# Delta rule on 32x32 blocks: the inverse's doubling products with four row and column groups

## The chip, the cores and the metric

The kernel runs on one core of a Trainium2 chip. The metric is the device time in microseconds (us) of one execution of the whole program, the median of three runs; a smaller number is better. A profile is one execution taken by the hardware profiler. Its engines are PE (TensorE's matmuls) and PEld (its weight loads, which overlap the matmuls), DVE (VectorE), ACT (ScalarE), POOL (GpSimd), and SP, which here issues DMAs only.

## The reference

One hybrid decoder layer: a combined projection, latent attention and a gated delta rule side by side, an output projection, and a gated convolutional feed-forward part. The change is in the delta rule alone. There the sequence is cut in chunks of 64 tokens, 33 of them, for four heads; for each chunk and head a unit lower triangular 64x64 matrix is inverted, and the state goes from chunk to chunk:

```
a_strict = jnp.einsum("bhnid,bhnjd->bhnij", k_beta, k) * decay * strict
t_inv = lax.linalg.triangular_solve(eye + a_strict, ..., lower=True, unit_diagonal=True)
u = t_inv @ v_beta;  w = t_inv @ (k_beta * exp(g))
...
v_new = u_c - w_c @ S
o = (q_c * exp(g_c)) @ S + qk_c @ v_new
S = S * exp(g_last) + (k_c * exp(g_last - g_c)).T @ v_new
```

`q` and `k` are divided by the root of their own square sums before this. All is float32.

## The kernel before

The program is a row of stages; stage_delta is the one that is changed. It lies between the short convolution and the attention, at about 693 to 1012 us of the profiled execution. It handles two chunks (`c` = 0, 1) at a time, which is called a tile here: 17 tiles, `t`. In a tile there are four units: two chunks times two pairs of heads. A unit holds two 64x64 matrices, one head on partitions 0 to 63 and one on 64 to 127 (`HALVES`).

The inverse is built by doubling. `xx` starts as the identity less the 2x2 blocks, as itself (half 0) and transposed (half 1). Each of five levels `lv` takes the off-diagonal blocks of its size from `nt[lv-1]` and forms, per head, P = `nt`·X (`first(lv)`, L1723), which ACT copies from the PSUM tile `pX` to `pr` (L1585), then X·P and its transpose (`second(lv)`, L1737 and L1739), which DVE adds to `xx` (L1641). Only then can the next level's `first` start. Levels 1 to 4 double blocks up to 32x32 and so touch nothing outside the 32x32 diagonal blocks of a matrix; level 5 fills the lower left 32x32 corner. The kernel before runs every product on the full 64x64 of a head, two heads side by side. ACT, DVE and PE do each level for chunk 0 and then for chunk 1.

Every engine runs a list of parts that `plain` writes out in a fixed order, tile after tile, with no loop left; a part stands with an offset, as (1, turn), the next tile's transpose. Engines meet in semaphores alone, so a part that waits holds all that stands behind it on its engine. PE's order in a tile is the last `plain` of the listing: between the products of the levels stand those of the state (`predict` L1770, `update` L1783, `outputs` L1796 and L1800, of the tile before), the next tile's `products` (L1699) and `turn` (L1709), the square sums of q of the tile after it (`q_norm`, L1688) and at the end `final` (L1750, L1755), which multiplies the inverse with v and k. DVE's order puts `state` (L1667, four instructions) ahead of the adds of level 2 and of level 5. ACT's order puts `turned` (L1579), the squares (L1543, L1544), the decays (L1567) and the copy of level 5 in one row, and then L1573 and `out(1)` (L1594), for whose end `final` waits.

Of the kernel before, what the change touches and what calls it, by code (L numbers as in the profile page):

```python
# [13 lines left out]
P = 128  # L14
# [784 lines left out]
def gates(nc, ctx, A, S, bank, ident, id_made):  # L799
# [32 lines left out]
    def load(pool):  # L832
# [3 lines left out]
        for hh in range(2):  # L836
            pool.dma_start(ab[hh * C2:hh * C2 + C2, 1:CHUNKS, :],
                          rows[N_META:L, :].rearrange("(c i) e -> i c e", i=CHUNK)).then_inc(loaded, 16)
            pool.dma_start(ab[hh * C2 + DN_PAD:hh * C2 + C2, 0, :], rows[0:N_META, :]).then_inc(loaded, 16)
        pool.dma_start(bias[:, :], A["dn_dt_bias"][0:1, :].to_broadcast([P, HEADS])).then_inc(loaded, 16)  # L840
# [10 lines left out]
    def masks_made(pool):  # L851
# [11 lines left out]
        for m in (tri, same, *only):  # L863
            step(pool.memset(m, 1.0))
        keep(only[0], [[0, P]], C2 - 1, -1)
        keep(only[1], [[0, P]], -C2, 1)
        keep(tri, [[1, P]], 0, -1)
# [466 lines left out]
GLB, NGC, ED, BETA = range(4)  # L1334
KINDS = 4
C2 = P // 2
HALVES = (slice(0, C2), slice(C2, P))
Q_LOG = -0.5 * float(np.log(P))


def stage_delta(nc, A, S):


    with ExitStack() as ctx:
        r = Room(nc, ctx, "dn")
        UH = UNITS * C2
        STEPS = LEVELS - 1
        LOADS = 3
        level_of, ident, off, eps, q_log, ones = (S[f"dn_{x}"] for x in ("level", "ident", "off", "eps", "q_log", "ones"))
# [6 lines left out]
        sqq = r.sb("sqq", [P, 2, HEADS, C2])  # L1356
# [12 lines left out]
        xx = [r.sb(f"xx{i}", [P, UNITS, 2, C2]) for i in range(2)]  # L1369
        nt = [r.sb(f"nt{i}", [P, STEPS, UNITS, C2]) for i in range(2)]  # L1370
        pr = r.sb("pr", [P, UNITS, C2])
# [5 lines left out]
        st = [r.sb(f"st{i}", [P, HEADS, P]) for i in range(2)]  # L1377
# [3 lines left out]
        pB = r.ps("pB", [P, 512])  # L1381
        pX = [r.ps(f"pX{i}", [P, 512]) for i in range(2)]
# [2 lines left out]
        pW = r.ps("pW", [P, 512])  # L1385
        pP = [p[:, 0:P].rearrange("p (u n) -> p u n", n=C2) for p in pX]
        pQ = [p[:, P:3 * P].rearrange("p (u x n) -> p u x n", u=2, x=2) for p in pX]
        pO, pV = pU[:, 0:2, :], pW[:, 0:2 * P].rearrange("p (g n) -> p g n", g=2)

        state_clear, loaded = r.sem("state_clear"), [S["dn_loaded0"]] + r.sems("loaded", LOADS - 1)  # L1390
        squared, qn_done, sums, logs, roots = (r.sems(x) for x in ("squared", "qn_done", "sums", "logs", "roots"))
# [217 lines left out]
        @block.vector  # L1609
        def _(dve):  # L1610
            dve.wait_ge(state_clear, 1)

            def square_sums(t, s, u):
                dve.wait_ge(squared[s], u + 1)
                dve.wait_ge(logs[s], u)
                dve.tensor_reduce(ss[s][:, 0:UNITS], sqk[:, :, :], AX.X, ALU.add)
                dve.wait_ge(qn_done[s], u + 1)
                dve.tensor_copy(ss[s][:, UNITS:], pB[:, UH:UH + UNITS]).then_inc(sums[s], 1)

            def strict(t, s, u):  # L1620
                dve.wait_ge(dec_strict[s], u + 1)
                dve.wait_ge(kk[s], u + 1)
                dve.wait_ge(x0_ready[1 - s], u + s)
                dve.wait_ge(bt_done[1 - s], u + s)
                dve.tensor_tensor(nn[:, 0, :, :], pK[:, :, 0, :], dec[:, 0, :, :], ALU.mult).then_inc(n_ready[s], 1)

            def attention(t, s, u):
                dve.wait_ge(dec_causal[s], u + 1)
                dve.wait_ge(o_done[1], t - 1) if t > 1 else None
                dve.tensor_tensor(qk[s][:, :, :], pK[:, :, 1, :], dec[:, 1, :, :], ALU.mult).then_inc(qk_ready[s], 1)  # L1630

            def level(lv):
                def run(t, s, u):
                    for c in range(2):
                        dve.wait_ge(q_done[c], STEPS * t + lv)
                        if lv == 1:
                            dve.wait_ge(x1_ready[s], u + 1)
                        x, q = xx[s][:, 2 * c:2 * c + 2, :, :], pQ[c]
                        if lv == STEPS:
                            x, q = x[:, :, 1, :], q[:, :, 1, :]  # L1640
                        dve.tensor_tensor(x, q, x, ALU.add).then_inc(x_step[c], 1)  # L1641
                return run

            def u_part(t, s, u):
                dve.wait_ge(u_done[s], 2 * u + 2)
                dve.tensor_copy(uu[s][:, :, :], pU[:, :, :]).then_inc(u_out[s], 1)

            def values(c):
                def run(t, s, u):
                    if c == 0:  # L1650
                        dve.wait_ge(u_out[s], u + 1)
                    dve.wait_ge(ws[c], t + 1)
                    dve.wait_ge(o_done[c], t)
                    dve.tensor_tensor(vn[c][:, :, :], uu[s][:, 2 * c:2 * c + 2, :], pV, ALU.subtract).then_inc(v_ready[c], 1)
                return run

            def state(c):
                def run(t, s, u):
                    dve.wait_ge(ks[c], t + 1)
                    if c == 0:  # L1660
                        dve.wait_ge(o_done[1], t)
                    else:
                        dve.wait_ge(o_done[0], t + 1)
                    dve.wait_ge(s_ready[1 - c], t + c)
                    for gg in range(2):
                        for hh in range(2):
                            o = dve.scalar_tensor_tensor(  # L1667
                                out=st[1 - c][:, 2 * gg + hh, :], in0=st[c][:, 2 * gg + hh, :],
                                scalar=egl[:, bass.ds(2 * t + c, 1), gg, hh], in1=pS[hh][:, gg, :],
                                op0=ALU.mult, op1=ALU.add)  # L1670
                    o.then_inc(s_ready[c], 1)
                return run

            plain(DT, (-1, values(0)), (0, level(1)), (-1, state(0)), (0, level(2)), (1, strict), (0, level(3)),
                  (-1, values(1)), (0, level(4)), (-1, state(1)), (0, level(5)), (2, square_sums), (1, attention), (0, u_part))

        @block.tensor
        def _(pe):
            pe.wait_ge(state_clear, 1)

            def q_norm(t, s, u):
                pe.wait_ge(squared[s], u + 1)
                pe.wait_ge(sums[1 - s], u + s)
                if t >= 1:
                    pe.wait_ge(bt_out[1 - s], u + s)
                for un in range(UNITS):
                    c, gg = un // 2, un % 2
                    m = pe.matmul(pB[:, UH + un:UH + un + 1], sqq[:, c, 2 * gg:2 * gg + 2, :].rearrange("p h i -> p (h i)"),  # L1688
                                  ones[:, :], start=True, stop=True)
                m.then_inc(qn_done[s], 1)  # L1690

            def products(t, s, u):
# [19 lines left out]
            def first(lv):  # L1712
                def run(t, s, u):
                    if lv == 1:
                        pe.wait_ge(x0_ready[s], u + 1)
                    pe.wait_ge(nt_ready[s], STEPS * u + lv)
                    for c in range(2):
                        pe.wait_ge(x_step[c], STEPS * t + lv - 1)
                        if STEPS * t + lv > 1:
                            pe.wait_ge(p_out[c], STEPS * t + lv - 1)  # L1720
                        for un in (2 * c, 2 * c + 1):
                            for rows in HALVES:
                                m = pe.matmul(pP[c][rows, un % 2, :], nt[s][rows, lv - 1, un, :], xx[s][rows, un, 0, :],  # L1723
                                              start=True, stop=True)
                        m.then_inc(p_done[c], 1)
                return run

            def second(lv):
                def run(t, s, u):
                    if lv == 1:  # L1730
                        pe.wait_ge(x1_ready[s], u + 1)
                    for c in range(2):
                        pe.wait_ge(p_out[c], STEPS * t + lv)
                        for un in (2 * c, 2 * c + 1):
                            if lv < STEPS:
                                for rows in HALVES:
                                    pe.matmul(pQ[c][rows, un % 2, 0, :], xx[s][rows, un, 1, :], pr[rows, un, :], start=True, stop=True)  # L1737
                            for rows in HALVES:
                                m = pe.matmul(pQ[c][rows, un % 2, 1, :], pr[rows, un, :], xx[s][rows, un, 1, :], start=True, stop=True)  # L1739
                        m.then_inc(q_done[c], 1)  # L1740
                return run

# [1928 lines left out]
```

## Time and profile before

| | before |
|---|---|
| median of 3 runs | 2991.72 us (2991.09 to 2991.76) |
| span of the profiled execution | 2990.1 us |
| PE busy over the span | 94% |
| mean granted TensorE clock | 0.974 of full speed |
| stage_delta, one tile in the steady part (835.92 to 853.48 us) | 17.56 us |

The profiled execution's span goes from its first to its last instruction; the median is 1.6 us above it. A row of the instruction list gives start, duration, engine, line, operation, what is written from what, shapes and count; merged rows of one kind cover several instructions. A form such as "64*64 64x64" is rows times columns of the weights, then the moving operand. A matmul's record goes from its start to the modelled end of its last result, so that records overlap, and a busy PE can still have room.

### The profile page before, as it was taken

Reading aid. Unit: us, or ns where it says so; the run is one execution under the profiler, and the core shown is the slowest. Engines: PE = TensorE matmul, PEld = TensorE weight load, DVE = VectorE, ACT = ScalarE, POOL = GpSimd, SP = SyncE. Lnnn points to the kernel's source line nnn. Section 1 sums busy time; section 2 is a strip of 40 time slices with the busy share of each in tenths; the row PEclk is TensorE's granted clock in tenths of the full one; section 3 lists DMA queues with packets and bytes.
Section 4 is the critical chain, followed back from the end, with each engine's and each line's share of the span. In section 5 each row is a group of like instructions: output and inputs, shape, how many; then the busy total and the mean of one; then the engine's idle time right before and its main releaser. Section 6 shows DMA issues by size and latency. Waiting matters only on the chain. (4 is left out here: it accounts for less than half of the span.)

```text
span 2990.1 us, 48834 instructions
## 1 busy us (share of the span) xinstructions
PE 2817.9 (94%) x18995; PEld 2440.4 (82%) x18995; DVE 1814.3 (61%) x2759; ACT 1181.2 (40%) x2210; POOL 1144.1 (38%) x1213
## 2 busy tenths in 40 slices
PE   7998979997999899998999599999999999999999
PEld 7997779996888688887788478888788888788887
DVE  3226834443555587777796677777887777543544
ACT  3226722223545365555443433333433333332321
POOL 2535930004776200001553456666666666100000
PEclk9999989997999899999999799999999999999999
DMA  8975953225454022221575633333533333654554
GB/s 269 354 251 171 263 166 111 67 74 130 108 147 87 22 75 91 85 68 40 179 246 164 216 93 105 95 103 94 190 105 99 101 105 97 240 170 146 192 167 142
DMA packets 403278, 421.07 MB, mean 141 GB/s; under 512 B 34075, under 2 KB 325995, under 8 KB 401000
## 3 DMA queue, kind: packets, MB, share of 16 engines
q1 hardware_dynamic: 368400, 298.61, 33.5%
q10 hardware_dynamic: 19944, 66.63, 6.8%
q0 software_dynamic: 14704, 52.69, 5.4%
q8 instruction: 153, 2.51, 0.3%
q14 instruction: 77, 0.63, 0.1%
HBM read 257.51 MB, written 160.34 MB: 140 GB/s over the span
## 5 line engine op out<-in xcount | busy, mean ns | idle before, releaser
L3526 PE MATMUL fu_pM<-fu_us_hi,fu_w_ring 128*128 128x512 f32 x2464 | 772.6, 393 | 15.2 <-DVE fu_us_lo L3361 14.3
L3526 PEld LDWEIGHTS fu_pM<-fu_us_hi,fu_w_ring 128*128 128x128 f32 x2464 | 466.3, 189 | 120.5 <-DVE fu_us_lo L3361 17.0
L3526 PE MATMUL fu_pM<-fu_us_lo,fu_w_ring 128*128 128x512 f32 x1232 | 482.8, 392 | 0.0
L3526 PEld LDWEIGHTS fu_pM<-fu_us_lo,fu_w_ring 128*128 128x128 f32 x1232 | 233.4, 189 | 47.8
L3262 ACT ACTIVATE fu_w_ring<-fu_sw 128x512 fp32r<-128x512 f32 x176 | 110.9, 631 | 325.3 <-PE fu_pM L3526 264.1
L3368 DVE TENSOR_TENSOR fu_w_ring<-fu_sw,fu_w_ring 128x512 fp32r<-128x512 f32 x132 | 139.4, 1056 | 65.4 <-ACT fu_w_ring L3262 65.3
L3368 DVE TENSOR_TENSOR fu_w_ring<-fu_w_raw,fu_w_ring 128x512 fp32r<-128x512 f32 x88 | 108.5, 1233 | 104.3 <-ACT fu_w_ring L3262 104.3
L2995 PE MATMUL fu_pM<-fu_us_hi,fu_w_ring 128*128 128x512 f32 x666 | 169.3, 391 | 1.3 <-DVE fu_w_ring L2918 1.3
L3262 ACT ACTIVATE fu_w_ring<-fu_w_raw 128x512 fp32r<-128x512 f32 x132 | 83.0, 629 | 191.3 <-PE fu_pM L3526 169.9
L3409 DVE SCALAR_TENSOR_TENSOR fu_acc<-fu_gb,fu_taps,fu_acc 128x1024 f32<-128x1024 f32 x88 | 133.0, 1513 | 37.7 <-ACT fu_acc L3303 36.9
L2075 ACT ACTIVATE at_pt_hi<-at_pT 128x512 fp32r<-128x512 f32 (+3 forms) x176 | 92.7, 539 | 143.6 <-PE at_pT L2340 142.7
L2918 DVE TENSOR_TENSOR fu_w_ring<-fu_w_ring 128x1408 fp32r<-128x1408 f32 x37 | 60.6, 1639 | 146.1 <-ACT fu_w_ring L2867 146.1
L2995 PEld LDWEIGHTS fu_pM<-fu_us_hi,fu_w_ring 128*128 128x128 f32 x666 | 125.8, 189 | 28.0 <-DVE fu_w_ring L2918 1.8
L2995 PE MATMUL fu_pM<-fu_us_lo,fu_w_ring 128*128 128x512 f32 x555 | 144.4, 392 | 4.0 <-DVE fu_w_ring L2918 4.0
L3219 POOL TENSOR_TENSOR fu_w_ring<-fu_w_raw,fu_w_ring 128x512 fp32r<-128x512 f32 x44 | 60.3, 1370 | 227.1 <-ACT fu_w_ring L3262 227.1
L2209 DVE TENSOR_TENSOR at_pt_lo<-at_pT,at_pt_hi 128x512 fp32r<-128x512 f32 (+3 forms) x176 | 106.2, 615 | 52.8 <-ACT at_pt_hi L2075 51.6
L2995 PEld LDWEIGHTS fu_pM<-fu_us_lo,fu_w_ring 128*128 128x128 f32 x555 | 105.1, 190 | 26.3 <-DVE fu_w_ring L2918 4.4
L2867 ACT ACTIVATE fu_w_ring<-fu_w_ring 128x1408 fp32r<-128x1408 f32 x37 | 51.0, 1379 | 182.7 <-PE fu_pM L2995 157.5
L1641 DVE TENSOR_TENSOR dn_xx<-dn_pX,dn_xx 128x256 f32<-128x256 f32 (+1 forms) x170 | 65.1, 397 | 78.1 <-PE dn_pX L1739 75.8
L2340 PE MATMUL at_pT<-id_ident,at_row 128*128 128x128 f32 x608 | 94.1, 276 | 13.5 <-ACT at_row L2067 11.8
L1469 POOL MEMSET dn_st<- 128x512 f32 x1 | 0.5, 524 | 276.3 <-POOLq L1017 276.3
L3219 POOL TENSOR_TENSOR fu_w_ring<-fu_sw,fu_w_ring 128x512 fp32r<-128x512 f32 x44 | 77.0, 1750 | 66.2 <-ACT fu_w_ring L3262 66.2
(539 smaller groups left out, 7141.5 us busy)
## 6 DMA issues: line engine op xcount, KB each, us to landing
fu_w_ring<-scr_gs ACTq DMA_DIRECT2D x37, 704.0 KB, 4.6
fu_w_raw<-in_w_gate SPq DMA_DIRECT2D x22, 1024.0 KB, 5.4
fu_w_raw<-in_w_up SPq DMA_DIRECT2D x22, 1024.0 KB, 5.4
scr_gs<-fu_sg SPq DMA_DIRECT2D x84, 256.0 KB, 3.0
scr_gs<-fu_acc SPq DMA_DIRECT2D x63, 256.0 KB, 2.9
fu_us_lo<-scr_gs ACTq DMA_DIRECT2D x19, 704.0 KB, 4.6
pj_wd<-in_w_down POOLq DMA_DIRECT2D x11, 1024.0 KB, 9.3
scr_td<-pj_td POOLq DMA_DIRECT2D x11, 1024.0 KB, 8.0
```

What stands on the lines that cost most here:

```text
L1641: dve.tensor_tensor(x, q, x, ALU.add).then_inc(x_step[c], 1)
L2075: act.activation(pt_hi[x % NPX][:, at:GW], pT[TURN[n, m] % NPT][:, :, :].rearrange("p i n -> p (i n)")[:, at:GW], ACT.Copy).then_inc(hi_do ...
L2209: dve.tensor_tensor(pt_lo[x % NPX][:, at:GW], pT[TURN[n, m] % NPT][:, :, :].rearrange("p i n -> p (i n)")[:, at:GW], f(pt_hi[x % NPX][:, a ...
L2340: t = pe.transpose(pT[x % NPT][:, i, :], rows[n % 2][i][:, at:at + P], ident[:, :])
L2867: act.activation(a_hi[s], f(a_lo[s]), ACT.Copy).then_inc(a_half, 1)
L2918: dve.tensor_tensor(a_lo[s], f(a_lo[s]), f(a_hi[s]), ALU.subtract).then_inc(a_ready, 1)
L2995: m = pe.matmul(pM[(U + e) % BANKS][:, :], a[s][:, j, :], x[c][j], start=(j == 0 and n_pass == 0), stop=(j == PAIRS - 1 and n_pass == 2))
L3219: pool.tensor_tensor(w_lo[q % RING][:, :, :], operand(ph % 2, i), f(w_hi[q % RING][:, :, :]), ALU.subtract).then_inc(w_ready_pool, 1)
L3262: act.activation(w_hi[q % RING][:, :, :], operand(m, i), ACT.Copy).then_inc(w_half, 1)
L3368: dve.tensor_tensor(w_lo[q % RING][:, :, :], operand(ph % 2, i), f(w_hi[q % RING][:, :, :]), ALU.subtract).then_inc(w_ready, 1)
L3409: dve.scalar_tensor_tensor(out=out, in0=gb[:, row, j:j + 2 * B], scalar=tap, in1=out, op0=ALU.mult, op1=ALU.add).then_inc(convolved[row] i ...
L3526: p = pe.matmul(bank(2 * n + m, i)[:, :], a[:, k, :], x[:, k, :], start=(k == 0 and n_pass == 0), stop=(k == HALVES_K - 1 and n_pass == 2))
```

## The change

Levels 1 to 4 run each product on the four 32x32 diagonal blocks of the 128 partitions (`BLOCKS`: block b has rows and columns of the array from 32b on), where two 64x64 blocks stood. Level 5 runs its two products on the 32x32 corner of each head alone (`CORNERS`), and writes the second to a PSUM region of its own, `pE`. Since DVE and ACT still read whole 64x64 regions, two products of zeros clear both banks of `pX` at the stage's start. `q_norm` is written as two products of 64 weight columns per unit, one for each half of the output partitions, where one of 128 columns stood.

```diff
@@ stage_delta
+        pE = [p[:, 3 * P:4 * P].rearrange("p (u n) -> p u n", n=C2) for p in pX]
+        BLOCKS = [(slice(b * QT, b * QT + QT), slice(b % 2 * QT, b % 2 * QT + QT)) for b in range(P // QT)]
+        CORNERS = [(BLOCKS[2 * hh], BLOCKS[2 * hh + 1]) for hh in range(2)]
...
@@ def level (DVE)
-                            x, q = x[:, :, 1, :], q[:, :, 1, :]
+                            x, q = x[:, :, 1, :], pE[c]
...
@@ def _(pe)
             pe.wait_ge(state_clear, 1)
+            for bank in pX:
+                pe.matmul(bank[:, :], st[0][:, 0, :], st[0][:, :, :].rearrange("p h d -> p (h d)"), start=True, stop=True)
...
@@ def q_norm
-                    m = pe.matmul(pB[:, UH + un:UH + un + 1], sqq[:, c, 2 * gg:2 * gg + 2, :].rearrange("p h i -> p (h i)"),
-                                  ones[:, :], start=True, stop=True)
+                    for hh, rows in enumerate(HALVES):
+                        m = pe.matmul(pB[rows, UH + un:UH + un + 1], sqq[:, c, 2 * gg + hh, :], ones[:, :], start=True, stop=True)
...
@@ def first
-                            for rows in HALVES:
-                                m = pe.matmul(pP[c][rows, un % 2, :], nt[s][rows, lv - 1, un, :], xx[s][rows, un, 0, :],
-                                              start=True, stop=True)
+                            if lv < STEPS:
+                                for rows, cols in BLOCKS:
+                                    m = pe.matmul(pP[c][rows, un % 2, cols], nt[s][rows, lv - 1, un, cols], xx[s][rows, un, 0, cols],
+                                                  start=True, stop=True)
+                            else:
+                                for (top, left), (low, right) in CORNERS:
+                                    m = pe.matmul(pP[c][low, un % 2, left], nt[s][top, lv - 1, un, right], xx[s][top, un, 0, left],
+                                                  start=True, stop=True)
...
@@ def second
-                                for rows in HALVES:
-                                    pe.matmul(pQ[c][rows, un % 2, 0, :], xx[s][rows, un, 1, :], pr[rows, un, :], start=True, stop=True)
-                            for rows in HALVES:
-                                m = pe.matmul(pQ[c][rows, un % 2, 1, :], pr[rows, un, :], xx[s][rows, un, 1, :], start=True, stop=True)
+                                for rows, cols in BLOCKS:
+                                    pe.matmul(pQ[c][rows, un % 2, 0, cols], xx[s][rows, un, 1, cols], pr[rows, un, cols],
+                                              start=True, stop=True)
+                                for rows, cols in BLOCKS:
+                                    m = pe.matmul(pQ[c][rows, un % 2, 1, cols], pr[rows, un, cols], xx[s][rows, un, 1, cols],
+                                                  start=True, stop=True)
+                            else:
+                                for (top, left), (low, right) in CORNERS:
+                                    m = pe.matmul(pE[c][top, un % 2, right], pr[low, un, left], xx[s][low, un, 1, right],
+                                                  start=True, stop=True)
```

On PE, level 4 with `turn` between its two halves: `first` writes `dn_pX` from `dn_nt`, `turn` writes `dn_pB`, and of `second` the first unit is shown. Before:

```order
L1723 MATMUL dn_pX<-dn_xx,dn_nt 64x64 x8
L1709 MATMUL dn_pB<-cd_ident,dn_nn 64x64 x8
L1737 MATMUL dn_pX<-dn_pr,dn_xx 64x64 x2
L1739 MATMUL dn_pX<-dn_xx,dn_pr 64x64 x2
L1737 MATMUL dn_pX<-dn_pr,dn_xx 64x64 x2
```

The same place now:

```order
L1730 MATMUL dn_pX<-dn_xx,dn_nt 32x32 x16
L1715 MATMUL dn_pB<-cd_ident,dn_nn 64x64 x8
L1748 MATMUL dn_pX<-dn_pr,dn_xx 32x32 x4
L1751 MATMUL dn_pX<-dn_xx,dn_pr 32x32 x4
L1748 MATMUL dn_pX<-dn_pr,dn_xx 32x32 x4
```

Nothing changes its place; each product of two halves is now four blocks, and `turn`, which stays at 64x64, stands between groups of another size.

On PE, level 5 and the end of a tile: `outputs` writes `dn_pU` (twice), `second(5)` writes `dn_pX`, then `q_norm` writes `dn_pB` and `final` starts with `dn_pU`. Before:

```order
L1723 MATMUL dn_pX<-dn_xx,dn_nt 64x64 x8
L1796 MATMUL dn_pU<-dn_st,dn_qt 64x128 x4
L1800 MATMUL dn_pU<-dn_vn,dn_qk 64x128 x4
L1739 MATMUL dn_pX<-dn_xx,dn_pr 64x64 x8
L1688 MATMUL dn_pB<-cd_ones,dn_sqq 128x1 x4
L1750 MATMUL dn_pU<-dn_vb,dn_xx 64x128 x8
```

The same place now:

```order
L1734 MATMUL dn_pX<-dn_xx,dn_nt 32x32 x8
L1813 MATMUL dn_pU<-dn_st,dn_qt 64x128 x4
L1817 MATMUL dn_pU<-dn_vn,dn_qk 64x128 x4
L1755 MATMUL dn_pX<-dn_xx,dn_pr 32x32 x8
L1695 MATMUL dn_pB<-cd_ones,dn_sqq 64x1 x8
L1767 MATMUL dn_pU<-dn_vb,dn_xx 64x128 x8
```

Level 5 keeps its eight products and has them smaller; `q_norm` has eight in place of four.

## Rows read from the trace of the kernel before

**Rows 1.** Busy us of PE, PEld, DVE, ACT, POOL; granted clock; DMA; two stretches.

```profile
770.00:810.00 40.00, 39.46 (x834) 34.47 (x836) 20.77 (x59) 18.51 (x66) 29.62 (x44) 1.00 0.53 124
835.90:853.46 17.56, 17.29 (x362) 15.06 (x360) 9.04 (x25) 8.69 (x31) 12.49 (x19) 1.00 0.57 144
```

**Rows 2.** Waits within that one tile: us in total, times, longest.

```profile
ACT dn_pr L1585 <- PE dn_pX L1723: 4.6, 4, 2.8
DVE dn_xx L1641 <- PE dn_pX L1739: 4.0, 4, 1.8
```

**Rows 3.** PE in order of time, one tile: start, duration, instruction, count.

```profile
835.92 0.68 PE L1723 MATMUL dn_pX<-dn_xx,dn_nt 64*64 64x64 f32 x16
838.68 0.87 PE L1723 MATMUL dn_pX<-dn_xx,dn_nt 64*64 64x64 f32 x16
842.23 0.68 PE L1723 MATMUL dn_pX<-dn_xx,dn_nt 64*64 64x64 f32 x16
842.84 0.66 PE L1796 MATMUL dn_pU<-dn_st,dn_qt 128*64 128x128 f32 x8
843.43 0.65 PE L1800 MATMUL dn_pU<-dn_vn,dn_qk 64*64 64x128 f32 x8
844.03 0.28 PE L1739 MATMUL dn_pX<-dn_xx,dn_pr 64*64 64x64 f32 x4
...
844.73 0.28 PE L1739 MATMUL dn_pX<-dn_xx,dn_pr 64*64 64x64 f32 x4
845.53 0.68 PE L1723 MATMUL dn_pX<-dn_xx,dn_nt 64*64 64x64 f32 x16
848.19 0.68 PE L1723 MATMUL dn_pX<-dn_xx,dn_nt 64*64 64x64 f32 x16
850.43 1.05 PE L1688 MATMUL dn_pB<-cd_ones,dn_sqq 128*128 128x1 f32 x8
851.42 1.09 PE L1750 MATMUL dn_pU<-dn_vb,dn_xx 64*64 64x128 f32 x16
853.48 0.33 PE L1723 MATMUL dn_pX<-dn_xx,dn_nt 64*64 64x64 f32 x4
```

**Rows 4.** All products of L1723 in the stage: count, busy us, mean ns.

```profile
L1723 PE MATMUL dn_pX<-dn_xx,dn_nt 64*64 64x64 f32 x1360 | 63.1, 229 | 3.3 <-issue 1.2 <-DVE dn_xx L1641 0.3
```

**Rows 5.** PE and its loads in order of time, at four places.

```profile
850.43 0.97 PEld L1688 LDWEIGHTS dn_pB<-cd_ones,dn_sqq 128*128 128x128 f32 x8
852.44 0.97 PEld L1755 LDWEIGHTS dn_pS<-dn_xx,dn_kbg 64*128 64x128 f32 x16 [0.17 <-issue]
1035.99 1.06 PE L2388 MATMUL at_pO<-da_vm_raw,at_sm_turned 16*16 16x128 f32 x8 [0.30 <-ACT at_sm_turned L2130]
1684.39 1.07 PE L3538 MATMUL fu_pM<-fu_w_raw,fu_head 128*32 128x256 f32 x16
```

**Rows 6.** ACT and DVE in order of time, the same tile.

```profile
836.04 0.66 ACT L1602 ACTIVATE dn_wt<-dn_pS 128x256 f32<-128x256 f32 x2 [2.88 <-PE dn_pS L1755]
840.24 1.12 DVE L1667 SCALAR_TENSOR_TENSOR dn_st<-dn_st,cd_egl,dn_pS 128x128 f32<-128x128 f32 x4 [1.20 <-PE dn_pS L1783]
841.28 0.75 DVE L1641 TENSOR_TENSOR dn_xx<-dn_pX,dn_xx 128x256 f32<-128x256 f32 x2
846.73 0.39 ACT L1579 ACTIVATE dn_nn<-dn_pB 128x256 f32<-128x256 f32 x1 [0.19 <-PE dn_pB L1709]
850.09 0.63 ACT L1594 ACTIVATE dn_osb<-dn_pU,dn_qscale 128x128 f32<-128x128 f32 x2
```

**Rows 7.** The stage's start in order of time.

```profile
695.37 1.84 PE L1688 MATMUL dn_pB<-cd_ones,dn_sqq 128*128 128x1 f32 x8 [10.29 <-ACT dn_sqq L1544]
705.04 1.42 POOL L1479 TENSOR_TENSOR dn_offs<-dn_grow,cd_off 128x256 f32<-128x256 f32 x2 [4.29 <-DMA dn_gall<-scr_gcr]
```

**Rows 8.** Two stretches of tile 0, columns as in rows 1.

```profile
712.60:716.00 3.40, 1.75 (x44) 1.54 (x46) 0.55 (x3) 1.48 (x7) 3.40 (x8) 1.00 0.00 0
716.00:719.40 3.40, 3.40 (x48) 2.93 (x46) 0.75 (x2) 0.56 (x2) 3.40 (x5) 0.50 0.70 192
```

More of the change, by code:

```diff
@@ L1336 @@
 C2 = P // 2
+QT = P // 4
 HALVES = (slice(0, C2), slice(C2, P))
```

## The prediction

> **What bounds the kernel now.** The change touches stage_delta alone, so I read that stage. First the table of stretches: in the steady part PE is busy 39.46 of 40.00 us and 17.29 of 17.56 us in one tile, at the full clock [rows 1]; the other engines are busy about half the time or, POOL, 71%. Then the waits of that tile: the longest on ACT and DVE are for PE's products of the inverse, 4.6 and 4.0 us [rows 2]. PE orders the stage, and the tile takes 17.56 us, from one first product to the next [rows 3].
>
> A busy PE need not be full, since records overlap, so I need what a product costs. Each float32 product shows two passes: 680 products of L1723 give 1360 records [rows 4]. In a dense run, from 844.03 to 844.73, six groups of four passes start 0.70 us apart, 29.2 ns for each pass [rows 3]. Are two halves side by side in that? Eight loads of 128 weight columns on all rows take 0.97 us, and sixteen on alternating halves take 0.97 us too [rows 5]; eight passes of 128 columns on one small tile take 1.06 us [rows 5], sixteen on two halves 1.09 [rows 3]. So two halves run together, and the unit is a slot: one pass on both halves, 58.3 ns for 64 columns. Sixteen passes of 256 columns on four column groups take 1.07 us [rows 5], twice the columns of L1750 in the same time: four run together there.
>
> **The change, part by part.** *Products.* A tile's inverse has 112 products before: 224 passes, 112 slots, 6.53 us of PE. After, levels 1 to 4 have 192 products in 96 slots of four, and level 5 has 16 in 16 slots of two: 112 slots again, with half the weight and half the moving columns. No row shows a 32x32 slot. Its lower bound is half, 29.2 ns. Its upper bound is that passes never come faster than now: four times 29.2, 116.7 ns, and 58.3 at level 5. It is nearest to the four column groups, which keep pace with their columns; I take 36 ns, the half and some 7 ns for two more starts per slot (an estimate). Saved: 112 x 22.3 ns = 2.50 us of PE a tile.
>
> The Trainium skill speaks against this: "TensorEngine Tiling (Array Packing)", Instruction Overhead, gives each matmul some 60 cycles whatever its free size and says not to take a tiling factor from a dimension that is already small. By it 416 passes of 25 ns would be 10.4 us where 6.53 stood, about +4 us a tile (an estimate from that page). The rows above show passes on different parts of the array started together, so whether that floor is the engine's or one block's no row here settles. It is the first rival below.
>
> *q_norm.* Eight passes with 128 weight columns take about 0.97 us; sixteen with 64 are eight slots, 0.47 us by the slot above. Saved 0.45 us with the ends.
>
> *Sizes that change.* Where PE goes from one tile size to another it loses time: L1796 begins at 842.84 and L1800 at 843.43 [rows 3], 0.59 us for four slots of 109 ns (L1750's 128 columns), so 0.15 us. After the change `turn` stands alone at 64x64 between 32x32 groups, and L1800 no longer has the size of the products behind it: four more such steps, +0.60 us a tile.
>
> *Zeros.* Two products of 512 columns at the start, four passes. L3538's 256 columns give about 0.22 us a pass, so 0.9 us at half speed for 512, 3.5 us in all. They hold the first `q_norm` of 695.37 by 1.5 us or so; but tile 0 waits on POOL, which itself waited for a load until 705.04 [rows 7]. I cost them at nothing. Without that cover they cost 1.5 us. `pE` is as large as what DVE read; nothing.
>
> *Sum on PE:* 2.50 + 0.45 - 0.60 = 2.35 us a tile. Over 17 tiles 40 us: the ceiling, 2952 us.
>
> *What the path gives.* Once PE is quicker, the chain product, copy, product, add is bare in places, so I walk the tile, first product to first product of the levels [rows 3].
> - Level 1, 2.76 us. The second product starts after ACT's `wt` copies (836.04 on) and two more ACT steps [rows 6], not after the first. Only chunk 0's half of the second shortens what follows: -0.18.
> - Level 2, 3.55. `update` starts some 0.09 earlier still, then `state` on DVE, 1.12 us, and only behind it the adds at 841.28 [rows 6]. PE's second is 0.36 shorter, and the next tile's `products` fill most of the wait: the next first can start at about 841.6. -0.45.
> - Level 3, 3.30. Second -0.36, first -0.13, one more step of size +0.15: -0.34.
> - Level 4, 2.66. First -0.08, second -0.36, two steps of size, 0.06 for the copy: -0.19.
> - Level 5, 2.24. -0.18, +0.10, -0.13: -0.21.
> - `q_norm` to the next tile, 3.05. PE would give -0.38. But `final` (851.42) waits for ACT's `out(1)` (850.09 to 850.72), and ACT works in one row from `turned` (846.73) to it [rows 6], 3.99 us. That row starts when `turn` does, about 1.0 us earlier, so `final` starts at about 849.77: -0.28.
>
> Together -1.65, a tile of 15.9 us. The other 0.7 us of PE's gain turns into waits for ACT and DVE. A slot of 29.2 ns would give about -1.8, one of 44 ns -1.25; at 57 ns the products save 0.15 and, with `q_norm`, no more than the steps of size cost.
>
> Sixteen tile lengths stand between the 17 first products: 16 x 1.65 = 26.4 us. I take 3 off for a lower clock now and then (second rival): 23.4. The span becomes 2990.1 - 23.4 = 2966.7; the median lay 1.6 above the span, so 2968 us.
>
> **Rivals.**
> 1. *Passes stay at 29.2 ns each* (issue, not the array, sets the pace). Then 416 passes cost 12.1 us where 6.53 stood, +5.6 - 0.45 + 0.60 = +5.75 a tile, +92 us over 16: 3084. It decides once a slot of four takes over 57 ns. For it: no row has passes closer on average in a long run. Against it: four column groups at once [rows 5]. A slot between 50 and 60 ns would give within 10 us of before.
> 2. *The clock falls in the thin part.* In tile 0, PE busy for 1.75 of 3.40 us was followed by a half clock, at which 48 passes took 3.40 us [rows 8]. After the change PE is thinnest from the first product to `update`, some 3.3 us: I count 1.6 us of columns in it, 2.3 of 3.6 before. If the clock halves there in each tile, that work takes twice as long, up to 1.6 us: the whole gain, 2991. In half of the tiles, 2979. If it stays low through the stage, most of the 14.9 us of PE's work left in a tile (17.29 - 2.35) doubles: over 3100.
> 3. *The chain hides more than I walked.* If ACT and DVE start no earlier than now but for level 2 and the last part, about -0.7 a tile: 2980.
>
> **How the numbers follow.** A measurement here can tell about 0.2% (6 us) from no change. My forecast, four together and ACT's row the next bound, 2957 to 2975: 0.55. The third rival, 2975 to 2984: 0.12. The second, 2979 to 2992: 0.14, two in five of it within 0.2%. A slot near break-even, within some 10 us of before: 0.05. The first rival, or a clock that stays low: 0.14, slower. Faster is 0.55 + 0.12 + 0.08 + 0.01 = 0.76, same 0.06 + 0.03 = 0.09, slower 0.15. The range from 2955 (the ceiling less three) to 2996 leaves out the first rival and a little at the low end.
>
> **What would show it.** Right: 32x32 products in groups of four passes every 36 ns or so, some 15.9 us a tile, waits of PE for `dn_xx` and `dn_pr`, `final` waiting for `dn_osb`, and the clock at 1.00 through the steady part. Wrong: groups of four no closer than 58 ns (first rival); stretches of the stage at 0.50 (second); a tile above 16.5 us at the full clock with short products (third). The rest of the program should only start earlier.

## The result and the profile after

The changed kernel takes 3062.18 us (median of four runs, 3051.91 to 3064.01); the kernel before, timed beside it, 2991.74 (2991.09 to 2992.59). The ratio is 1.0231, 95% interval 1.0214 to 1.0248: slower by 2.3%, 94 us above the forecast and 66 us above its range. The profiled execution, the shortest of the four, took 3051.91 us, its span 3050.2. The span grew by 60.1 us, and all of it lies in stage_delta: from the start of the first tile's `products` to that of the last it takes 345.1 us, 284.9 before.

The view to open first is that of stretches, for the changed kernel: busy us of PE, PEld, DVE, ACT and POOL, then the granted clock, the DMA share and GB/s. The first row is the stretch of [rows 1], the second one tile, the others lie inside that tile.

```profile
770.00:810.00 40.00, 35.46 (x967) 29.42 (x964) 14.27 (x39) 13.14 (x50) 20.17 (x31) 0.65 0.39 86
905.86:926.98 21.12, 17.70 (x563) 14.35 (x561) 8.90 (x25) 8.60 (x31) 12.52 (x19) 0.84 0.47 122
910.70:914.10 3.40, 1.59 (x63) 1.38 (x63) 1.13 (x4) 0.00 (x0) 2.64 (x4) 1.00 0.74 206
914.10:917.50 3.40, 3.19 (x93) 2.34 (x83) 0.71 (x2) 1.07 (x4) 1.45 (x2) 0.50 0.83 170
917.50:920.90 3.40, 3.40 (x107) 2.82 (x107) 0.85 (x2) 0.83 (x4) 0.00 (x0) 0.50 0.35 96
```

Where the clock stood at 1.00 it is now 0.65 in the first row, and PE is idle for 4.54 us of 40 where it was idle for 0.54. A tile takes 21.12 us in place of 17.56, and holds 563 PE records and 561 of PEld in place of 362 and 360 (a float32 product shows as four records: two passes, each with a weight load on PEld). The third row is the one to keep in mind: at the full clock PE was busy for only 1.59 of 3.40 us, and after it come two stretches at half clock.

Why was PE idle there? The waits of that tile (us in total, times, longest):

```profile
ACT dn_pr L1589 <- PE dn_pX L1730: 7.0, 2, 4.7
DVE dn_xx L1645 <- PE dn_pX L1751: 6.8, 5, 2.6
...
PE dn_pX L1748 <- issue: 2.5, 2, 2.2
```

ACT and DVE wait for PE's products longer than before [rows 2], although each is shorter, and PE's longest wait is put down to "issue", that is, to nothing that the profile shows. PE in order of time around it (start, duration, instruction, count, idle before):

```profile
909.05 0.71 PE L1800 MATMUL dn_pS<-dn_vn,dn_kd 64*128 64x128 f32 x8
909.70 0.26 PE L1748 MATMUL dn_pX<-dn_pr,dn_xx 32*32 32x32 f32 x8
...
910.11 0.21 PE L1751 MATMUL dn_pX<-dn_xx,dn_pr 32*32 32x32 f32 x2
912.51 0.23 PE L1748 MATMUL dn_pX<-dn_pr,dn_xx 32*32 32x32 f32 x4 [2.20 <-issue]
```

The stop of 2.20 us falls in the middle of one chunk's second products, where the program has no wait at all: the products before and after it are of one unit, and their operands were ready before the chunk began. What moved then is seen in the view of the DMA queues (packets, MB, share of 16 engines). Three rows of it: the stretch from 910.0 to 911.2, then 730 to 970 in this kernel, then 730 to 970 in the kernel before:

```profile
q8 instruction: 1, 0.02, 5.5%
q8 instruction: 49, 0.80, 1.4%
q8 instruction: 39, 0.64, 1.1%
```

Queue q8 carries instructions. Its one packet from 910.0 to 911.2, 16,384 bytes, started at 910.06 and took 1.05 us; PE ran another 13 records, stopped at 910.31 and went on at 912.51. That is the pattern everywhere: between 860 and 1000 PE stops 12 times for over 0.6 us, and each stop ends 2.3 to 3.0 us after the start of such a packet. Between 730 and 970 the queue carried 49 packets where the kernel before had 39, for 12,272 and 9,814 records of PE and PEld: 250 and 252 records a packet.

So the reading to test: PE's program is delivered in packets of some 250 records, a packet can be used 2.3 to 3.0 us after its transfer starts, and a row of blocks is used up sooner. Theory A says that this is the loss and that the half clock comes behind these stops. Theory B is the prediction's second rival: the blocks leave PE too few columns, and the clock falls for that.

### The profile page after: what moved, and what is told of

Same layout as the page of the kernel before. It is cut to its first block and busy times, and to the rows that moved or that the text cites. A ratio compares the mean times of both kernels' runs of the same rounds, so it can differ in the third digit from the quotient of the medians.

```text
span 3050.2 us, 55642 instructions
## 1 busy us (share of the span) xinstructions
PE 2835.7 (93%) x22399; PEld 2437.7 (80%) x22399; DVE 1808.6 (59%) x2759; ACT 1180.1 (39%) x2210; POOL 1144.8 (38%) x1213
```

## The experiments

All are timed against the kernel before on the same chip; the pattern of the first two is a square: the changed kernel has thin products (few columns) and many instructions, the kernel before thick ones and few, and each of these two has one of each.

**Thin products, few instructions.** The changed kernel, with one product of 64 rows and 32 columns for each half in place of two blocks (the same in `second`, and at level 5 in place of the corners, whose result DVE then reads from `pQ` again):

```diff
-for rows, cols in BLOCKS:
-    m = pe.matmul(pP[c][rows, un % 2, cols], nt[s][rows, lv - 1, un, cols], xx[s][rows, un, 0, cols], start=True, stop=True)
+for hh, rows in enumerate(HALVES):
+    top, left = BLOCKS[2 * hh]
+    m = pe.matmul(pP[c][top, un % 2, left], nt[s][rows, lv - 1, un, left], xx[s][rows, un, 0, left], start=True, stop=True)
```

> The changed kernel, but each 64x64 product of the inverse is cut to its upper left 32x32 (64 rows, 32 weight columns, 32 moving columns, one product for each half as before): about half of PE's columns in the products, as in the changed kernel, but 112 products a tile and not 208. It leaves out three quarters of each product's output, so the inverse is not computed. Theory A (instructions arrive too slowly: PE runs dry in the middle of groups, and these stops take the clock down): no stop over 0.6 us within a group in the steady part, granted clock 1.00 in nearly all of the stage, a tile of 15.5 to 16.5 us, 2955 to 2980 us. Theory B (the clock falls because the products keep too few columns busy, with or without stops): no stops either, but the clock at half in a third of the stage or more, a tile over 17.5 us, over 2995 us.

It takes 2973.26 us, ratio 0.9935 (0.992 to 0.995). The stretches, of the steady part and of one tile, of this kernel:

```profile
730.00:970.00 240.00, 219.60 (x5496) 180.55 (x5494) 127.70 (x373) 125.23 (x454) 185.50 (x280) 0.98 0.50 116
828.32:843.69 15.37, 14.43 (x375) 11.89 (x369) 8.53 (x26) 8.47 (x31) 12.49 (x20) 1.00 0.73 166
```

With the changed kernel's thin work the clock is 0.98, and a tile without a long stop takes 15.37 us. Theory B's fall does not come. Theory A was not quite right either: it expected no long stop, and there are seven over 0.6 us between 730 and 970. Shorter products alone use up instructions faster (738 records in 15.37 us, where 722 took 17.56), and the tiles are 15.4 to 17.8 us long.

**Thick products, many instructions.** The kernel before, each product cut into two by its weight columns, so that four run side by side on 64 rows and 32 columns:

```diff
-for rows in HALVES:
-    m = pe.matmul(pP[c][rows, un % 2, :], nt[s][rows, lv - 1, un, :], xx[s][rows, un, 0, :], start=True, stop=True)
+for (rows, cols), half in zip(BLOCKS, (HALVES[0], HALVES[0], HALVES[1], HALVES[1])):
+    m = pe.matmul(pP[c][rows, un % 2, :], nt[s][half, lv - 1, un, cols], xx[s][half, un, 0, :], start=True, stop=True)
```

> The kernel before, each 64x64 product of the inverse cut into two by its weight columns (64 rows, 32 weight columns, all 64 moving columns; four run side by side): the computation and PE's columns are those of before, but there are 224 products a tile in place of 112, so PE has some 1190 records a tile in place of 740. Theory A (instructions arrive too slowly): stops of 1 to 3 us in the middle of groups, one or two a tile, more than 20 us over the stage, and stretches at half clock behind them: 3020 to 3080 us. Theory B (too few columns): the clock stays at 1.00, no more than the steps of tile size are lost (0.3 to 0.6 us a tile): 2992 to 3003 us.

It takes 3054.98 us, ratio 1.021 (1.0196 to 1.0224): theory A's case. PE in order of time, a run of its second products, and then the stretch of the steady part:

```profile
830.18 0.29 PE L1739 MATMUL dn_pX<-dn_pr,dn_xx 64*32 64x64 f32 x8
830.29 0.29 PE L1742 MATMUL dn_pX<-dn_xx,dn_pr 64*32 64x64 f32 x8
...
830.52 0.27 PE L1742 MATMUL dn_pX<-dn_xx,dn_pr 64*32 64x64 f32 x3
831.54 0.31 PE L1742 MATMUL dn_pX<-dn_xx,dn_pr 64*32 64x64 f32 x5 [0.75 <-issue]
```

```profile
730.00:970.00 240.00, 209.19 (x6480) 170.89 (x6480) 100.97 (x276) 98.21 (x346) 137.94 (x209) 0.96 0.43 100
```

Eight passes take 0.11 us, 57 ns for four side by side with 64 columns: the array does its work at the pace of before. The same computation with the same columns is 2.1% slower because each product comes in two pieces, and PE stops in the middle of a group of eight. From the first `products` to the last it takes 52.5 us more than the kernel before, and PE's idle time put down to "issue" between 690 and 1080 is 35 us more: most of this loss is stops. The rest is left for the clock (0.96) and the steps of tile size, which this kernel has too.

**The sums of squares alone.** The kernel before with the change to `q_norm`:

```diff
-m = pe.matmul(pB[:, UH + un:UH + un + 1], sqq[:, c, 2 * gg:2 * gg + 2, :].rearrange("p h i -> p (h i)"), ones[:, :], start=True, stop=True)
+for hh, rows in enumerate(HALVES):
+    m = pe.matmul(pB[rows, UH + un:UH + un + 1], sqq[:, c, 2 * gg + hh, :], ones[:, :], start=True, stop=True)
```

> The kernel before with the sums of squares alone on two column groups (8 products of 64 weight columns in place of 4 of 128), all products on 64x64. Both theories: no change of the clock and no stops. By the walk of the prediction, PE is 0.45 us quicker behind level 5, and the final products then wait for the copy of the outputs on ACT: between nothing and 0.4 us a tile, 2984 to 2992 us.

It takes 2983.98 us, ratio 0.9973 (0.9964 to 0.9982), at the better end of the expectation: a tile of 17.13 us against 17.55, by the starts of `products`, and no stop over 0.6 us in the steady part.

**Corners and sums of squares.** The changed kernel with levels 1 to 4 on 64x64 again (in `first`, and the same in `second`):

```diff
 if lv < STEPS:
-    for rows, cols in BLOCKS:
-        m = pe.matmul(pP[c][rows, un % 2, cols], nt[s][rows, lv - 1, un, cols], xx[s][rows, un, 0, cols], start=True, stop=True)
+    for rows in HALVES:
+        m = pe.matmul(pP[c][rows, un % 2, :], nt[s][rows, lv - 1, un, :], xx[s][rows, un, 0, :], start=True, stop=True)
```

> The changed kernel with levels 1 to 4 on 64x64 again: only level 5 runs on 32x32 corners (16 products, as many as before) and the sums of squares run on two column groups (8 products in place of 4). Theory A: 16 more records a tile bring no stops; level 5 saves 16 slots of some 22 to 26 ns, 0.35 to 0.4 us, the sums of squares up to 0.45, and the new steps of size take about half of that back; 0.2 to 0.5 us a tile, 2980 to 2988 us, the clock at 1.00. Theory B: the thinner end of the tile already takes the clock down in some tiles: 2990 us or more.

It takes 2981.85 us, ratio 0.9968 (0.9956 to 0.9981), the fastest here but for the thin kernel, which leaves work out. The interval overlaps that of the sums of squares alone; the profile tells the corners' share, 16.80 us against 17.13 in the commonest tile, 17.01 against 17.34 on average. Its stretch, and the end of one tile in PE's order of time:

```profile
730.00:970.00 240.00, 235.45 (x5222) 202.01 (x5222) 126.44 (x356) 120.66 (x435) 177.34 (x269) 1.00 0.49 115
```

```profile
857.41 0.44 PE L1734 MATMUL dn_pX<-dn_xx,dn_nt 32*32 32x32 f32 x16
858.95 0.44 PE L1755 MATMUL dn_pX<-dn_xx,dn_pr 32*32 32x32 f32 x16
859.32 0.63 PE L1695 MATMUL dn_pB<-cd_ones,dn_sqq 128*64 128x1 f32 x16
```

Both products of level 5 take 0.44 us in place of the first's 0.68 [rows 3], the sums of squares 0.63 in place of 1.05. So those two parts of the change are worth having; what is left to blame is the blocks of levels 1 to 4.

**How many instructions are too many.** Four kernels stand between the corners kernel and the changed one. They put the blocks of 32x32 back for a part of levels 1 to 4, here for the second products of level 3:

```diff
-if lv < STEPS:
+if lv in (3,):
+    for rows, cols in BLOCKS:
+        pe.matmul(pQ[c][rows, un % 2, 0, cols], xx[s][rows, un, 1, cols], pr[rows, un, cols], start=True, stop=True)
+    for rows, cols in BLOCKS:
+        m = pe.matmul(pQ[c][rows, un % 2, 1, cols], pr[rows, un, cols], xx[s][rows, un, 1, cols], start=True, stop=True)
+elif lv < STEPS:
     for rows in HALVES:
...
```

> The corners kernel (level 5 on corners, sums of squares on two column groups) and, at levels 1 to 4, 32x32 blocks for the first products alone: 32 products more, some 884 records a tile against 756 (and 1124 in the changed kernel). Theory A (a packet of 256 instructions comes some 2.4 us after it is asked for, and PE stops where it has used up the half it still has): in the first products the block groups are followed by a wait for ACT, so few stops, 0 to 10 us in all; the eight slots a level save 0.2 us each, part of it on the path: 2970 to 2990 us. Theory B (too few columns): less than a tenth of PE's columns are gone, the clock stays, no stops: 2968 to 2978 us.

> The corners kernel and, at levels 1 to 4, 32x32 blocks for the second products alone: 64 products more, some 1012 records a tile, 64 of them in a row in each chunk. Theory A: stops of 1 to 3 us in most tiles, 20 to 40 us in all, and stretches at half clock: 3000 to 3045 us. Theory B: twice the columns of the first products are gone; if that alone takes the clock, stretches at half clock without stops ahead of them; if not, 2960 to 2975 us.

> The corners kernel and 32x32 blocks for the second products of levels 2 and 4 alone: 32 products more, as many records a tile (884) as with all first products on blocks, but in two runs of 128. Theory A: if the count in a short time matters, more stops than with the first products, 5 to 20 us in all; what the blocks save on the path (0.3 to 0.7 us a tile) is about given back: 2972 to 2995 us. Theory B: the clock stays and nothing stops: 2968 to 2978 us.

> The corners kernel and 32x32 blocks for the second products of level 3 alone: 16 products more, 820 records a tile, one run of 128 a tile between the outputs and the predict group, which run at 25 ns a record or slower. Theory A: a stop only where a packet is asked for just ahead of the run, in some tiles, under 8 us in all; the blocks save up to 0.36 us a tile: 2973 to 2985 us. Theory B: no stops, 2975 to 2980 us.

In the kernel with blocks in the first products alone, the second products read beside the diagonal blocks what level 5 of the tile before left in `pP`, which changes the computation but no instruction. The expectations' counts are 18 to 20 a tile higher, as they take in waits (but not the 1124 of the changed kernel); the table has records of PE and PEld alone, 722 before [rows 1] and 4 for each product added. Clock and stops are those of the stretch 730 to 970, stops being PE's idle time put down to "issue". Short idle times, most of them ahead of a first product, are in that column too: stops of over 0.6 us come to 6.9 us in the thin kernel, 7.5 to 7.7 in the three behind it, then 29.6, 27.3 (changed) and 26.3, and to nothing in the first three rows. Each ratio is to the kernel before on the chip of that run, where its median was 2992.83 (the first four experiments) or 2992.49 us (the last four).

| kernel | records a tile | time, us | ratio (95%) | clock | stops, us |
|---|---|---|---|---|---|
| before | 722 | 2991.74 | 1 | 0.99 | 0.2 |
| sums of squares alone | 738 | 2983.98 | 0.9973 (0.9964 to 0.9982) | 1.00 | 0.2 |
| corners, sums of squares | 738 | 2981.85 | 0.9968 (0.9956 to 0.9981) | 1.00 | 0.8 |
| thin, few | 738 | 2973.26 | 0.9935 (0.992 to 0.995) | 0.98 | 13.8 |
| second, level 3 | 802 | 2989.10 | 0.9997 (0.9989 to 1.0006) | 0.99 | 8.6 |
| first, levels 1 to 4 | 866 | 2986.46 | 0.9981 (0.9972 to 0.9989) | 0.96 | 9.2 |
| second, levels 2 and 4 | 866 | 2986.82 | 0.9982 (0.9974 to 0.9991) | 0.96 | 10.8 |
| second, levels 1 to 4 | 994 | 3038.66 | 1.0149 (1.0134 to 1.0165) | 0.83 | 33.4 |
| changed | 1122 | 3062.18 | 1.0231 (1.0214 to 1.0248) | 0.77 | 31.9 |
| thick, many | 1170 | 3054.98 | 1.021 (1.0196 to 1.0224) | 0.96 | 27.2 |

Theory A's case again, with two misses. The second products of level 3 alone were expected between 2973 and 2985 us with under 8 us of stops, and took 2989 with 8.6: already 64 records a tile bring seven stops of over 0.6 us between 730 and 970 and give back what the corners had won. And the two kernels with 866 records do not differ, so the count in a tile told more here than how I had spread it. Theory B has no account of the first of these: only the second products of one level are thinner there, the clock is 0.99, and the gain is gone all the same.

Two things in these traces settle more than the times do. First, where PE stops. The seven kernels with stops have 84 of over 0.6 us between 730 and 970. From one such stop to the next in the same kernel there is always a whole number of packets, with 248 to 252 records of PE and PEld for each (in the changed kernel, for example, 252, 252, 754, 1004, 1258), and just as many packets start their transfer in between. So PE stops at the end of a packet, when the next one is not there yet, and each stop ends 2.2 to 3.2 us after that packet's start. After a stop, the next transfer starts only 1.0 to 3.4 us later: while PE uses one packet, only the one after it is on its way. Where two stops lay one packet apart, they were 3.7 us apart at the least.

Second, when the clock falls. In the ten kernels it fell from full to half speed 27 times between 730 and 970, ten of them in the changed kernel. Each time PE was in a stop of over 0.6 us or had ended one at most 2.5 us before; in the three kernels without such stops it never fell there. Theory B's fall without stops is in none of these stretches.

## Why the prediction was wrong, point by point

- **The slot: right.** 36 ns taken (29.2, and 7 for two more starts, which no row showed), bounds 29.2 and 116.7; 32 measured. Four groups of eight passes of the changed kernel at the full clock, start and duration:

```profile
896.16 0.24 PE L1751 MATMUL dn_pX<-dn_xx,dn_pr 32*32 32x32 f32 x8
896.23 0.24 PE L1748 MATMUL dn_pX<-dn_pr,dn_xx 32*32 32x32 f32 x8
896.29 0.24 PE L1751 MATMUL dn_pX<-dn_xx,dn_pr 32*32 32x32 f32 x8
896.35 0.25 PE L1748 MATMUL dn_pX<-dn_pr,dn_xx 32*32 32x32 f32 x6
```

  From 896.16 to 896.35 six slots go by in 0.19 us: 32 ns for four passes, 8 ns for one. The first rival falls: passes on different blocks do not hold each other to 29.2 ns. The Trainium skill's "TensorEngine Tiling (Array Packing)", Instruction Overhead, gives each matmul some 60 cycles; as a price for each of several products side by side it does not agree with these rows.
- **The sums of squares: right on PE, too low on the path.** 0.45 us forecast for PE, 1.05 against 0.63 found; the walk let 0.28 of it through, and the tile gained 0.42.
- **The walk: right in kind, a little too careful.** It gave 15.9 us a tile. The thin kernel, with as many slots and the same steps of tile size, runs a tile without long stops in 15.37. Sixteen tiles shorter by 2.18 us each would be 35 us, 2957 in all. By that kernel, which starts two products side by side where the changed one starts four, this much of the gain is there on the array; in the changed kernel itself no run shows it free of stops.
- **The zeros: right.** They took 3.78 us (3.5 forecast), and PE's first level product starts at 708.64, at 708.73 before.
- **The step that failed: "112 slots again, with half the weight and half the moving columns".** The sum costed the products as slots of the array and nothing else. It saw 208 products where 112 stood and never asked how their instructions reach PE. "Issue" came in only as a pace of the passes (the first rival), and that pace was fine. What took its place was not a price for each pass but stops at the ends of instruction packets: 15 of over 0.6 us for the 49 packets between 730 and 970, 27.3 us, and with the short ones 31.9 us in some 11 tiles, 2.9 us a tile, more than the 1.65 us that the walk had won. The half clock behind them, and what waits for PE then, took about as much again, by subtraction (next point).
- **The clock: taken as 3 us, and the second rival had its cause wrong.** That rival let the clock fall wherever PE is thin. The thin kernel has that thinness and the clock at 0.98; it is 0.77 in the changed kernel, where thinness and many long stops meet. In the tile shown above the stop comes first, the half clock after it, and so with all ten falls between 730 and 970. Stops with thick products take it only to 0.96, but those stops are shorter too: none over 1.9 us, where seven of the changed kernel's 15 last over 2.0. The price of the clock by itself was not measured: a tile of the changed kernel is 21.57 us long on average (by the starts of `products`), 6.2 above 15.37, of which idle time put down to "issue" is 2.9, and the remaining 3.3 is left for the half clock and what waits for PE then, by subtraction.
- **The third rival** can't be judged from the changed kernel. In the thin kernel PE is busy for 14.43 of 15.37 us; the chain hid less than that rival feared.

The Trainium skill does bear on the failed step, though the prediction did not draw on it there: "Runtime: NRT & Kernel Launch", Instruction fetch mechanics, says that instructions come in blocks of 16 KiB, 256 of them, fetched ahead, and that the cost of crossing a block is mostly hidden because the sequencer dispatches more slowly than blocks arrive. The size agrees (16,384 bytes, some 250 records and the waits among them). That the crossing is hidden holds in the kernel before, 0.2 us of stops in 240, at 24 ns a record (17.56 us by 722). It does not hold here, where a dense row of blocks has eight records every 32 ns.

What stays open: why a packet's transfer starts now 1.0 and now 3.4 us after PE has begun the packet ahead of it, and why none starts sooner. In the twelve stops between 860 and 1000 PE ran from 0 to 142 records between the packet's start and the stop, and in two of them the packet started only after PE had stopped. Open too is what takes the clock as far down as 0.77: the square of four kernels shows that neither thin products with few stops (0.98) nor thick products with short stops (0.96) do, but it does not separate thinness from the length of the stops, and no kernel here held the clock up under the changed kernel's stops.

## What to carry to other kernels

Before splitting products into smaller ones that run side by side, count instructions as well as columns. Here each product is four records, a packet holds some 250, and where PE had to wait for two packets running, the second came 3.7 to 6.3 us after the first; so a row of short products is safe only where the 250 records of a packet last about that long. In the kernel before they last 6.1 us on average, and PE had no stop. In the profile of such a kernel look for idle time of PE put down to "issue" in the middle of a group, and for a count of instruction packets that has risen. Take those parts of such a change that add next to no instructions: here corners and column groups in `q_norm` gave 0.3%, and the blocks gave all of it back.

## What the runs showed of the hardware

- Four 32x32 products side by side start 8 ns apart, 32 ns for four of 32 columns at the full clock; four of 64x32 with 64 columns take 57 ns.
- PE's instructions came in packets of 16,384 bytes, one for 247 to 252 records of PE and PEld in each of the ten kernels, 0.9 to 1.8 us in transfer.
- Between 730 and 970, all 84 stops of over 0.6 us in seven kernels ended 2.2 to 3.2 us after a packet's start and lay whole packets apart (248 to 252 records each); after each, the next packet started 1.0 to 3.4 us later. In the kernel before, with 39 packets there, none stopped PE that long.
- In the changed kernel a stretch with PE busy for 1.59 of 3.40 us at the full clock was followed by two at half clock; in the thin kernel a tile with PE busy for 14.43 of 15.37 us ran at 1.00. All 27 falls of the clock between 730 and 970, over the ten kernels, came in a stop or at most 2.5 us after its end.
